# Root mean square norms by quarters: ScalarE's own sums under the root, gate product beside the squares, block 0 turned first

## The chip, the cores and the metric

One core of a Trainium2 chip runs the whole program. The metric is the device time of one launch in microseconds (us), the median of several runs. The engines are TensorE (PE; its weight loads are PEld), VectorE (DVE), ScalarE (ACT), GpSimd (POOL) and SyncE (SP), which issues most DMAs. TensorE writes only to PSUM, here eight banks of 128 x 512 f32, `PS[0]` to `PS[7]`.

## What is computed

Two transformer blocks over 256 tokens of width 1024, in f32, each a token mixer and then a mixture of experts (64 experts with 8 per token in the first, 32 with 2 per token in the second). What matters here are the norms around them:

```python
def rms_norm(x, g):
    return x * rsqrt(mean(x * x, axis=-1) + EPS) * g

# first block
x = x + gate0 * rms_norm(token_mixer(...), g_post_mix)      # norm 0
h = rms_norm(x, g_pre_ffn) * (1 + scale) + shift            # norm 1, then the router and the experts
x = x + gate1 * rms_norm(moe(h), g_post_ffn)                # norm 2
# second block
h = rms_norm(x, norm1_g) * (1 + scale1) + shift1            # norm 3
x = x + gate_mix * (mixed @ w_out)
h = rms_norm(x, norm2_g) * (1 + scale2) + shift2            # norm 4, then the router and the experts
x = x + gate_ffn * hier_moe(h)
return rms_norm(x, norm_f_g)                                # norm 5
```

## The kernel before

**Data.** `x` and `xn` hold the 256 tokens as two blocks `b` of 128 partitions by 1024 columns. A quarter is one block's half of 512 columns: quarter n is block n // 2, half n % 2. `hT` is the normalised and modulated `x` turned to features by tokens, eight slices `k` of 128 features; TensorE turns 128 x 128 pieces of `xn` into `PS[0]` to `PS[3]`, two slices to a bank, and VectorE (slices 0, 1, 4, 5) and ScalarE (2, 3, 6, 7) bring them to `hT` with scale `am` and shift `modc`. `gate` and `gate2` hold the gate rows broadcast over partitions.

**Order.** Each engine has its own program, written out by hand, and runs it in order. `Steps` (the helper `step`) adds to a semaphore behind an instruction and, unless told `wait=False`, makes the same engine wait for it before going on. Between engines there are named semaphores: `norm_in` (a block of `x` or `xn` is ready to be squared), `norm_sq` (ScalarE has squared it), `norm_ms` (VectorE has made mean + EPS), `norm_root` (ScalarE has the root), `xnorm_ready`, `modT` (a bank is turned), `ada_ready`, `y_done` (a quarter of the experts' sum is whole in PSUM), `stream_used`, `e1_gateup` and others (a weight buffer is free again).

**A norm of one block** goes: ScalarE squares 1024 columns and sums them (`norm`, L791), VectorE scales the sum and adds EPS (L1973), ScalarE takes the root (L793), VectorE the reciprocal (L1975). For a branch's norm (`add_branch`, norms 0 and 2) VectorE then multiplies by root and gate row (L1982) and adds to `x` (L1984), block after block; for a norm ahead of a projection (`modulated`, norms 1, 3, 4) it scales `x` into `xn` (L1997), both blocks, and TensorE turns both (L1208) when `xnorm_ready` says that the second is there. The last norm multiplies by its gain (L2336), and SyncE stores each block.

**The four places,** named as in the prediction: A, between the mixer's output projection (`mixed_out`, L1173) with three gate rows (`gate_rows`, L952, copied by ScalarE at L853) and the first router (L1225): norms 0 and 1. B, between the first layer's experts (L1378 closes the sums in PSUM, L2175 copies them out) and the second block's input projection (L1461): norms 2 and 3. C, between the second block's output projection (L1577; VectorE multiplies by the gate and adds at L1989, L1990) and its router: norm 4. D, behind the last expert: norm 5 and the store (L624).

**Weights.** SyncE issues the loads in order into a ring of twelve slots of 1 MB (`load_piece`, L536), later into three buffers (`load2`, L598), each when TensorE has used what lies there.

## Time and profile before

| | us |
|---|---|
| median of 3 runs | 1522.45 |
| lowest and highest | 1518.49, 1523.02 |
| profiled execution, first to last instruction (its span, and the only time that it has) | 1523.0 |
| TensorE busy | 1241.4 (82%) |
| weight loads of TensorE busy | 628.8 (41%) |
| VectorE busy | 360.9 (24%) |
| ScalarE busy | 181.5 (12%) |
| HBM read | 505.25 MB, 332 GB/s over the span |
| granted TensorE clock, mean | 0.901 |

The page is one execution as the hardware profiler saw it. A clock of 1.00 is 2.4 GHz and of 0.50 is 1.2 GHz. A timeline row gives the start, the time from first start to last end of the instructions merged in it, how many they are, and in brackets the idle time before them and who ended it. A stretch row gives busy time with instruction counts. The line numbers are those of the kernel before.

### The profile page before, as it was taken

How to read it: one execution, taken by the hardware profiler on the slowest of the kernel's cores; microseconds unless marked ns; L12 is line 12 of the kernel's file. 1: busy time of each engine (PE TensorE's matmuls, PEld its weight loads, DVE VectorE, ACT ScalarE, POOL GpSimd, SP SyncE). 2: the span in 40 equal slices, each digit the busy share in tenths (PEclk: the TensorE clock that was granted, in tenths of full speed). 3: DMA queues.
4: the chain of work that ended last, by engine and by line, in shares of the span. 5: the costliest groups of instructions: out<-in, count | busy, mean ns of one | idle time of the engine just before them, and what ended most of it. 6: DMA issues, size and time to landing. Idle time of an engine off the chain costs nothing.

```text
span 1523.0 us, 21627 instructions
## 1 busy us (share of the span) xinstructions
PE 1241.4 (82%) x8940; PEld 628.8 (41%) x8940; DVE 360.9 (24%) x932; ACT 181.5 (12%) x346; POOL 95.3 (6%) x125
## 2 busy tenths in 40 slices
PE   4999889899998989989796999887675675675764
PEld 2763335555555545545446544453221221221211
DVE  1498653611111101111113153323000000000002
ACT  1210200411111111111112012021000000000001
POOL 2398000000000000000001000000000000000000
PEclk9999979999999989999998999987788877778877
DMA  9875993269999999999967324445999999999993
GB/s 338 311 281 193 395 412 139 111 262 405 419 420 420 420 420 420 420 421 419 420 255 267 151 89 168 183 182 202 421 421 421 420 422 421 422 422 422 421 422 150
DMA packets 85980, 507.59 MB, mean 333 GB/s; under 512 B 8310, under 2 KB 9558, under 8 KB 36356
## 3 DMA queue, kind: packets, MB, share of 16 engines
q1 hardware_dynamic: 84804, 502.98, 80.9%
q0 software_dynamic: 944, 3.29, 0.7%
q8 instruction: 64, 1.05, 0.3%
q10 hardware_dynamic: 144, 0.07, 0.0%
q14 instruction: 24, 0.20, 0.0%
HBM read 505.25 MB, written 1.06 MB: 332 GB/s over the span
## 4 chain that ended last, share of the span: by engine, by line
PE 56%; DMA 32%; DVE 8%; SPq 2%; issue 2%; ACT 1%; DVEq 0%; ACTq 0%
DMA W<-in_w_expert_down 12%; DMA W<-in_w_expert_up 10%; PE PS L1432 10%; DMA W<-in_we_up 7%; PE PS L1300 5%; PE PS L1443 5%; PE PS L1287 4%; PE PS L1501 4%; PE PS L1597 3%; PE PS L1609 3%; PE PS L936 2%; DMA W<-in_w_ada 2%; PE PS L1173 2%; PE PS L1461 2%; PE PS L1577 2%; PE PS L1562 2%
## 5 line engine op out<-in xcount | busy, mean ns | idle before, releaser
L1597 PE MATMUL PS<-W,scr 128*32 128x512 f32 x1024 | 178.3, 862 | 121.6 <-DMA W<-in_w_expert_up 61.5
L1432 PE MATMUL PS<-W,scr 128*32 128x256 f32 (+1 forms) x2752 | 191.6, 400 | 30.9 <-DMA W<-in_we_up 26.6
L2098 DVE TENSOR_TENSOR scr<-scr,PS 128x256 f32<-128x256 f32 (+1 forms) x33 | 23.5, 712 | 664.5 <-PE PS L1597 386.4
L1432 PEld LDWEIGHTS PS<-W,scr 128*32 128x32 f32 (+1 forms) x2752 | 116.0, 120 | 113.8 <-issue 64.3
L1597 PEld LDWEIGHTS PS<-W,scr 128*32 128x32 f32 x1024 | 40.8, 150 | 257.5 <-issue 112.0
L1300 PE MATMUL PS<-scr 128*128 128x512 f32 x264 | 122.1, 605 | 2.5 <-ACT scr L824 2.5
L1609 PE MATMUL PS<-W,scr 128*32 128x512 f32 x512 | 72.7, 719 | 37.5 <-DMA W<-in_w_expert_down 36.6
L1287 PE MATMUL PS<-scr 128*128 128x128 bf16 x1584 | 93.8, 219 | 0.0
L1287 PEld LDWEIGHTS PS<-scr 128*128 128x128 bf16 x1584 | 91.2, 98 | 1.5 <-issue 1.1
L1443 PE MATMUL PS<-W,scr 128*32 128x512 f32 (+1 forms) x688 | 91.1, 596 | 0.7 <-DVE scr L2101 0.7
L813 ACT COPY scr<-PS 128x512 f32<-128x512 f32 x66 | 38.7, 586 | 437.8 <-PE PS L1287 437.8
L1300 PEld LDWEIGHTS PS<-scr 128*128 128x128 f32 x264 | 47.4, 189 | 67.7 <-issue 67.7
L824 ACT COPY scr<-PS 128x512 f32<-128x512 f32 x66 | 35.4, 589 | 211.9 <-PE PS L1609 128.2
L1501 PE MATMUL PS<-W,hT 128*128 128x512 f32 x128 | 56.0, 595 | 0.0
L936 PE MATMUL PS<-W,sc 128*32 128x512 f32 x384 | 48.3, 647 | 6.8 <-DMA W<-in_w_ada 6.6
L1609 PEld LDWEIGHTS PS<-W,scr 128*32 128x32 f32 x512 | 17.7, 128 | 86.3 <-DMA W<-in_w_expert_down 43.8
L669 POOL TENSOR_SCALAR scr<-scr,convw 128x256 f32<-128x256 f32 x44 | 44.4, 1010 | 4.3
L1443 PEld LDWEIGHTS PS<-W,scr 128*32 128x32 f32 (+1 forms) x688 | 24.5, 114 | 47.5 <-issue 44.1
L818 ACT ACTIVATE scr<-PS 128x256 f32<-128x256 f32 (+1 forms) x33 | 14.4, 435 | 219.3 <-PE PS L1597 142.5
L2101 DVE COPY scr<-PS 128x256 f32<-128x256 f32 (+1 forms) x33 | 16.1, 489 | 97.7 <-PE PS L1318 97.7
L1501 PEld LDWEIGHTS PS<-W,hT 128*128 128x128 f32 x128 | 24.0, 190 | 30.0 <-issue 30.0
L683 POOL DMA_DIRECT2D scr<-bias_by_distance x1 | 0.9, 925 | 558.1 <-DVEq L2180 558.1
(410 smaller groups left out, 1172.6 us busy)
## 6 DMA issues: line engine op xcount, KB each, us to landing
W<-in_we_gate SPq DMA_DIRECT2D x64, 1024.0 KB, 19.2
W<-in_we_up SPq DMA_DIRECT2D x64, 1024.0 KB, 17.4
W<-in_we_down SPq DMA_DIRECT2D x64, 1024.0 KB, 20.7
W<-in_w_expert_gate SPq DMA_DIRECT2D x64, 1024.0 KB, 18.8
W<-in_w_expert_up SPq DMA_DIRECT2D x64, 1024.0 KB, 19.0
W<-in_w_expert_down SPq DMA_DIRECT2D x64, 1024.0 KB, 19.3
W<-in_w_ada SPq DMA_DIRECT2D x10, 4096.0 KB, 18.6
W<-in_w_in SPq DMA_DIRECT2D x5, 4096.0 KB, 13.8
```

The source lines that it names most:

```text
L669: step(g.tensor_scalar(tmp, upad[:, i, :, j:j + ROW], convw[:, 4 * j + i:4 * j + i + 1], None, ALU.mult))
L813: a.copy(hTe[:, 4 * q:4 * q + 4, :], PS[4 + q][:].rearrange("p (k s) -> p k s", k=4)).then_inc(S["x_hTe"], 1)
L824: a.copy(Y[:, h * 512:(h + 1) * 512], PS[6 + h][:]).then_inc(S["x_Y"], 1)
L936: last = mm(PS[5 + h][32 * j:32 * j + 32, :], sc[:, 2 * j + kk, 30 - row:62 - row], ada_w[n][:, 2 * j + kk, h * 512:(h + 1) * 512], start= ...
L1173: last = mm(PS[2 * b + h][:, :], mixT[:, k, b * P:(b + 1) * P], w_o[:, k, h * 512:(h + 1) * 512], start=(k == 4), stop=(k == 3))
L1287: last = mm(PS[4 + k // 4][:, (k % 4) * P:(k % 4 + 1) * P], hs[:, part, b, k * P:(k + 1) * P], Sb[:, b, :], start=(q == 0), stop=(q == NB ...
L1300: last = mm(PS[2 * b + h][:, :], Ct[:, b * P:(b + 1) * P], Y[:, h * 512:(h + 1) * 512], start=False, stop=False)
L1432: m = mm(PS[4 + kind][at:at + size, 0:F1], hTe[:, k, at:at + size], piece_view((g, kind, j))[:, k, :], start=(k == 0), stop=(k == KD - 1))
L1443: m = mm(PS[6 + h][at:at + size, :], aT[:, c, at:at + size], piece_view((g, 2, j))[:, c, h * 512:(h + 1) * 512], start=(c == 0), stop=(c = ...
L1501: last = mm(PS[6 + n % 2][:, :], hT[:, k, b * P:(b + 1) * P], w2k[2 + half][:, k, h * 512:(h + 1) * 512], start=(k == 0), stop=(k == KD - 1))
L1597: m = mm(PS[bank][j * CAP2:(j + 1) * CAP2, :], hTe[:, k, j * CAP2:(j + 1) * CAP2], gu2[piece][:, j, kk, :], start=(k == 0), stop=(k == KD ...
L1609: m = mm(PS[6 + h][j * CAP2:(j + 1) * CAP2, :], aT[:, c, j * CAP2:(j + 1) * CAP2], dn2[piece][:, j, cc, h * 512:(h + 1) * 512], start=(c = ...
```

## The change

- Each root is made by ScalarE from two quarters. `root_of` squares a quarter with scale 1/32 (so that the sum is already a mean over 1024), adds EPS to the first sum by an Identity with a bias column `epsc`, squares the second quarter, and takes the root of its sum with the first as bias. VectorE's scaling step and `norm_sq`, `norm_ms` are gone in these norms.
- `norm_in` and the new `branch_in` count quarters, so a quarter is squared when it is there.
- In norm 0 VectorE multiplies the branch by the gate row into `branch` (the upper half of `hT`'s words) while ScalarE squares it; root and addition to `x` are then one fused instruction per quarter (`add_scaled`). In norm 2 the gate product takes the place of the copy out of PSUM, ScalarE squares `PS[0]` and `PS[1]` straight from the banks while VectorE takes quarters 2 and 3, and VectorE takes quarters 0 and 1 once block 0's root is there.
- `normalised(n, b)` scales one block and signals it. TensorE's `turn_rows(n, b)` turns one block: in A block 0 goes between gate rows 3 and 1, in C ahead of the last quarter of the output projection.
- In A block 0 goes through both norms on VectorE before the third quarter of the projection is read.
- `root_table` has ScalarE take a root of a constant ahead of norms 2, 4 and 5.
- The output is stored by quarters, in four DMAs of 256 KB.

```diff
--- before.py
+++ after.py
@@ -306,6 +306,12 @@
         sel16 = sel32[:, 0:16]
         ada_bias = [gate[:, n, :] for n in range(2)]
         onec = small[:, 340:341]
+        epsc, spare = small[:, 440:441], small[:, 441:442]
+
+        squares = [[[small[:, at:at + 1] for at in (448 + 8 * n + 4 * b, 449 + 8 * n + 4 * b)] for b in range(NB)] for n in range(2)]
+        halfway = [[small[:, 450 + 8 * n + 4 * b:451 + 8 * n + 4 * b] for b in range(NB)] for n in range(2)]
+        roots = [[small[:, 451 + 8 * n + 4 * b:452 + 8 * n + 4 * b] for b in range(NB)] for n in range(2)]
+        branch = hT_words[:, D:2 * D]
         cvec = small[:, 376:400].rearrange("p (v k) -> p v k", v=3)
 
         rowd = {"post_mix": scr[:, 4096:5120], "post_ffn": scr[:, 11264:12288]}
@@ -619,10 +625,11 @@
 
             over_loads(2, ("w_expert_gate_2", "w_expert_up_2", "w_expert_down_2"))
 
-            for b in range(NB):
-                sp.wait_ge(S["out_ready"], b + 1)
-                sp.dma_start(out[0][b * P:(b + 1) * P, :], xn[:, b, :]).then_inc(S["stored"], 16)
-            sp.wait_ge(S["stored"], 16 + 16 * NB)
+            for n in range(4):
+                b, q = n // 2, slice(n % 2 * 512, n % 2 * 512 + 512)
+                sp.wait_ge(S["out_ready"], n + 1)
+                sp.dma_start(out[0][b * P:(b + 1) * P, q], xn[:, b, q]).then_inc(S["stored"], 16)
+            sp.wait_ge(S["stored"], 16 + 16 * 4)
 
 
         @block.gpsimd
...
@@ -785,12 +793,25 @@
                 mod_columns(bank, i, b, s, n == 2)
 
 
-            def norm(n, src):
-                for b in range(NB):
-                    act.wait_ge(S["norm_in"], 2 * n + b + 1)
-                    step(a.activation(hT_words[:, 0:D] if n < 2 else ada_rows[:], src[:, b, :], ACT.Square, accum_out=st[:, 24 + b:25 + b]), S["norm_sq"])
-                    act.wait_ge(S["norm_ms"], 2 * n + b + 5)
-                    step(a.activation(st[:, 26 + b:27 + b], st[:, 26 + b:27 + b], ACT.Sqrt), S["norm_root"])
+            def root_of(n, b, quarters, ready, first):
+
+                unused = hT_words[:, 0:512] if n < 2 else ada_rows[:, 0:512]
+                for h in range(2):
+                    act.wait_ge(S[ready], first + h)
+                    step(a.activation(unused, quarters[2 * b + h][:, 0:512], ACT.Square, scale=1.0 / 32, accum_out=squares[n % 2][b][h]))
+                    if h == 0:
+                        step(a.activation(halfway[n % 2][b], squares[n % 2][b][0], ACT.Identity, bias=epsc))
+                step(a.activation(roots[n % 2][b], squares[n % 2][b][1], ACT.Sqrt, bias=halfway[n % 2][b]), S["norm_root"])
+
+            x_quarter = [x[:, n // 2, n % 2 * 512:n % 2 * 512 + 512] for n in range(4)]
+            xn_quarter = [xn[:, n // 2, n % 2 * 512:n % 2 * 512 + 512] for n in range(4)]
+
+            def root_of_x(n, nth, b):
+                root_of(n, b, x_quarter, "norm_in", 4 * nth + 2 * b + 1)
+
+            def root_table():
+
+                step(a.activation(spare, onec, ACT.Sqrt))
 
             def split_h(L, part):
 
...
@@ -875,10 +898,11 @@
                 act.wait_ge(S["sh_gateup"], b + 1)
                 step(a.activation(sg_sh[:, b, :], PS[6 + b][:, 0:F1], ACT.Silu), S["sh_sg"], wait=False)
             experts(1, NG1, F1, 2)
-            norm(2, xn)
-
-
-            norm(3, x)
+            root_table()
+            root_of(2, 0, PS, "y_done", 1)
+            root_of(2, 1, PS, "branch_in", 5)
+            for b in range(NB):
+                root_of_x(3, 1, b)
             odd_banks_of_h(1, 1, 0, 2)
 
             for h in range(HEADS2):
...
@@ -1193,21 +1221,24 @@
                 last.then_inc(S["hmT"], 1)
             pe.wait_ge(S["mixT_m"], 2)
             mixed_out(0)
+            def turn_rows(n, b):
+
+                pe.wait_ge(S["xnorm_ready"], 2 * n + b + 3)
+                for k in range(KD):
+                    part = xn[:, b, k * P:(k + 1) * P] if n == 1 else every_kd(xn[:, b, :])[:, k, :]
+                    last = tr(PS[k // 2][:, (k % 2) * T + b * P:(k % 2) * T + (b + 1) * P], part, ident[:])
+                    if b and k % 2:
+                        last.then_inc(S["modT"], 1)
+
             pe.wait_ge(S["gates_made"], 1)
             gate_rows(2, (5, 6))
             gate_rows(3, (4, 7))
+
+            pe.wait_ge(S["branch_in"], 4)
+            turn_rows(0, 0)
             pe.wait_ge(S["ada_ready"], 5)
             gate_rows(1, (5, 6))
-
-            def modulated(n, src):
-
-                pe.wait_ge(S["xnorm_ready"], n + 3)
-                for k in range(KD):
-                    for b in range(NB):
-                        part = src[:, b, k * P:(k + 1) * P] if n == 1 else every_kd(src[:, b, :])[:, k, :]
-                        last = tr(PS[k // 2][:, (k % 2) * T + b * P:(k % 2) * T + (b + 1) * P], part, ident[:])
-                    if k % 2:
-                        last.then_inc(S["modT"], 1)
+            turn_rows(0, 1)
 
             def part_of_h(n, k):
 
...
@@ -1447,7 +1477,8 @@
             experts(1, NG1, F1, gate_and_up1, down1)
 
 
-            modulated(1, xn)
+            for b in range(NB):
+                turn_rows(1, b)
 
             def loaded2(i):
                 pe.wait_ge(S[f"stream2_loaded{i % 2}"], 16 * (i // 2 + 1) if i != 5 else 48)
@@ -1577,9 +1608,11 @@
                     last = mm(PS[4 + n][:, :], hT[:, k, b * P:(b + 1) * P], w2k[5][:, k, h * 512:(h + 1) * 512],
                               start=(k == 0), stop=(k == KD - 1))
                 last.then_inc(S["stream2_used"] if n == 3 else S["proj_mm"], 1)
-
-
-            modulated(2, xn)
+                if n == 2:
+                    turn_rows(2, 0)
+            turn_rows(2, 1)
+
+
             routed(2, 2, wr2, 36)
             pe.wait_ge(S["zraw_ready"], 1)
             ranks(2, E2)
@@ -1961,40 +1994,35 @@
             over_rows(1, E1)
             sort_keys()
 
-            norms = []
-
-            def next_norm():
-                norms.append(len(norms))
-                return norms[-1]
-
-            def root_mean_square(n, b):
-
-                dve.wait_ge(S["norm_sq"], 5 + 2 * n + b)
-                step(v.tensor_scalar(st[:, 26 + b:27 + b], st[:, 24 + b:25 + b], 1.0 / D, EPS, ALU.mult, ALU.add), S["norm_ms"])
-                dve.wait_ge(S["norm_root"], 5 + 2 * n + b)
-                step(v.reciprocal(st[:, 26 + b:27 + b], st[:, 26 + b:27 + b]))
-
-            def add_branch(gate_row):
-
-                n = next_norm()
-                for b in range(NB):
-                    root_mean_square(n, b)
-                    step(v.scalar_tensor_tensor(out=xn[:, b, :], in0=xn[:, b, :], scalar=st[:, 26 + b:27 + b],
-                                                in1=gate_row, op0=ALU.mult, op1=ALU.mult))
-                    step(v.tensor_tensor(x[:, b, :], x[:, b, :], xn[:, b, :], ALU.add), S["norm_in"])
+            ROOTS = [(0, 0), (1, 0), (0, 1), (1, 1)] + [(n, b) for n in range(2, 6) for b in range(NB)]
+
+            def inverse_root(n, b):
+
+                dve.wait_ge(S["norm_root"], 5 + ROOTS.index((n, b)))
+                inverse = st[:, 26 + b:27 + b]
+                step(v.reciprocal(inverse, roots[n % 2][b]))
+                return inverse
+
+            def add_scaled(n, b, product):
+
+                inverse = inverse_root(n, b)
+                for h in range(2):
+                    q = slice(h * 512, h * 512 + 512)
+                    step(v.scalar_tensor_tensor(out=x[:, b, q], in0=product[:, q], scalar=inverse, in1=x[:, b, q],
+                                                op0=ALU.mult, op1=ALU.add), S["norm_in"])
 
             def add_product(gate_row, n, bank):
 
                 b, q = n // 2, slice(n % 2 * 512, n % 2 * 512 + 512)
                 step(v.tensor_tensor(xn[:, b, q], bank[:], gate_row[:, q], ALU.mult))
-                step(v.tensor_tensor(x[:, b, q], x[:, b, q], xn[:, b, q], ALU.add), S["norm_in"] if n % 2 else None)
+                step(v.tensor_tensor(x[:, b, q], x[:, b, q], xn[:, b, q], ALU.add), S["norm_in"])
+
+            def normalised(n, b):
+
+                step(v.tensor_scalar(xn[:, b, :], x[:, b, :], inverse_root(n, b), None, ALU.mult), S["xnorm_ready"])
 
             def modulated(n, blk, sec, vec, gain):
 
-                norm = next_norm()
-                for b in range(NB):
-                    root_mean_square(norm, b)
-                    step(v.tensor_scalar(xn[:, b, :], x[:, b, :], st[:, 26 + b:27 + b], None, ALU.mult), S["xnorm_ready"] if b else None)
                 step(v.scalar_tensor_tensor(out=am[:, 0, :], in0=modc[:, blk, sec + 1, :, vec], scalar=1.0,
                                             in1=gain, op0=ALU.add, op1=ALU.mult), S["am_ready"])
                 for k in (0, 1, 4, 5):
@@ -2146,8 +2174,10 @@
                 for h in range(2):
                     dve.wait_ge(S["stream_used"], AT["w_out"] + 1) if b and h else dve.wait_ge(S["proj_mm"], 17 + 2 * b + h)
                     q = slice(h * 512, (h + 1) * 512)
-                    step(v.tensor_tensor(xn[:, b, q], PS[2 * b + h][:], rowv[:, q], ALU.add), S["norm_in"] if h else None)
-            add_branch(gate[:, 0, :])
+                    step(v.tensor_tensor(xn[:, b, q], PS[2 * b + h][:], rowv[:, q], ALU.add), S["branch_in"])
+                    step(v.tensor_tensor(branch[:, q], xn[:, b, q], gate[:, 0, q], ALU.mult))
+                add_scaled(0, b, branch)
+                normalised(1, b)
             modulated(0, 0, 2, 0, ffn_cols[:, FFN_G1, :])
 
             mixer_gate(1, 7)
@@ -2170,12 +2200,16 @@
             make_ranks(1, E1)
             experts(1, NG1, F1, 2)
 
-            for n in range(4):
+            for n in (2, 3, 0, 1):
                 dve.wait_ge(S["y_done"], n + 1)
-                step(v.tensor_copy(xn[:, n // 2, n % 2 * 512:n % 2 * 512 + 512], PS[n][:]), S["norm_in"] if n % 2 else None)
-            add_branch(gate[:, 1, :])
-
-
+                if n == 0:
+                    dve.wait_ge(S["norm_root"], 5 + ROOTS.index((2, 0)))
+                q = slice(n % 2 * 512, n % 2 * 512 + 512)
+                step(v.tensor_tensor(xn[:, n // 2, q], PS[n][:], gate[:, 1, q], ALU.mult), S["branch_in"] if n > 1 else None)
+            for b in range(NB):
+                add_scaled(2, b, xn[:, b, :])
+            for b in range(NB):
+                normalised(3, b)
             modulated(1, 1, 0, 2, cols[:, C_N1:C_N1 + 8])
             dve.sem_inc(S["x2_ready"], 1)
             for q in range(4):
@@ -2270,8 +2304,8 @@
             for n in range(4):
                 dve.wait_ge(S["proj_mm"], 23 + n) if n < 3 else dve.wait_ge(S["stream2_used"], 6)
                 add_product(gate2[:, 0, :], n, PS[4 + n])
-
-
+                if n % 2:
+                    normalised(4, n // 2)
             modulated(2, 1, 2, 2, ffn_cols[:, FFN_G2, :])
             dve.wait_ge(S["router_mm"], 2)
             zz = tmpr.rearrange("p b e -> p (b e)")[:, 0:72].rearrange("p (b n) -> p b n", b=NB)
@@ -2330,11 +2364,12 @@
                 add_product(gate2[:, 1, :], n, PS[n])
 
             dve.wait_ge(S["poolw_loaded"], 32)
-            norm = next_norm()
             for b in range(NB):
-                root_mean_square(norm, b)
-                step(v.scalar_tensor_tensor(out=xn[:, b, :], in0=x[:, b, :], scalar=st[:, 26 + b:27 + b], in1=rowf,
-                                            op0=ALU.mult, op1=ALU.mult), S["out_ready"])
+                inverse = inverse_root(5, b)
+                for h in range(2):
+                    q = slice(h * 512, h * 512 + 512)
+                    step(v.scalar_tensor_tensor(out=xn[:, b, q], in0=x[:, b, q], scalar=inverse, in1=rowf[:, q],
+                                                op0=ALU.mult, op1=ALU.mult), S["out_ready"])
 
 
 
```

## Rows read from the trace of the kernel before

**Rows 1.** The page's part 4: shares of the chain that ended last, by engine.

```profile
PE 56%; DMA 32%; DVE 8%; SPq 2%; issue 2%; ACT 1%; DVEq 0%; ACTq 0%
```

**Rows 2.** Stretches: busy us (instructions) of PE, PEld, DVE, ACT, POOL, granted clock, DMA, GB/s.

```profile
345.00:440.00 95.00, 95.00 (x1130) 54.04 (x1131) 14.12 (x59) 15.39 (x29) 0.00 (x0) 1.00 1.00 414
1060.00:1500.00 440.00, 285.31 (x1856) 89.31 (x1852) 22.45 (x48) 19.89 (x35) 0.00 (x0) 0.79 1.00 418
```

**Rows 3.** Timeline of SyncE's DMA queue: start us, us with waits between, instructions.

```profile
269.79 36.36 SPq L536 DMA_DIRECT2D W<-in_we_up  x2
```

**Rows 4.** Groups by shape: line, engine, operation, tiles, count, busy us, mean ns, idle before.

```profile
L895 ACT ACTIVATE scr<-scr 128x512 f32<-128x512 f32 x8 | 4.4, 618 | 4.8 <-DVE scr L2231 4.8
L888 ACT ACTIVATE scr<-scr,small 128x256 f32<-128x256 f32 x8 | 4.1, 508 | 0.3
L818 ACT ACTIVATE scr<-PS 128x256 f32<-128x256 f32 x25 | 9.6, 383 | 76.8 <-PE PS L1432 76.8
L793 ACT ACTIVATE small<-small 128x1 f32<-128x1 f32 x12 | 2.4, 203 | 14.6 <-DVE small L1973 14.5
L791 ACT ACTIVATION_READ_ACCUMULATOR ada_rows<-x 128x1 f32 x6 | 1.1, 187 | 0.0
L1982 DVE SCALAR_TENSOR_TENSOR xn<-xn,small,gate 128x1024 f32<-128x1024 f32 x4 | 5.1, 1284 | 0.1
L1984 DVE TENSOR_TENSOR x<-x,xn 128x1024 f32<-128x1024 f32 x4 | 4.9, 1226 | 0.1
```

**Rows 5.** Timelines of VectorE, ScalarE and TensorE in A: start us, us, idle before.

```profile
268.54 0.69 DVE L2149 TENSOR_TENSOR xn<-PS,scr 128x512 f32<-128x512 f32 x1 [2.74 <-PE PS L1173]
278.41 0.75 DVE L1997 TENSOR_SCALAR xn<-x,small 128x1024 f32<-128x1024 f32 x1
273.08 1.07 ACT L853 COPY gate<-PS 128x512 f32<-128x512 f32 x2
268.27 3.60 PE L952 MATMUL PS<-ada_rows,scr 128*128 128x512 f32 x8
274.21 1.98 PE L952 MATMUL PS<-ada_rows,scr 128*128 128x512 f32 x4 [2.34 <-ACT gate L853]
279.22 3.53 PE L1208 MATMUL PS<-ident,xn 128*128 128x128 f32 x16 [3.03 <-DVE xn L1997]
```

**Rows 6.** Stretches behind the waits of A and C, columns as in rows 2.

```profile
279.20:290.00 10.80, 10.78 (x69) 9.74 (x70) 6.27 (x20) 5.67 (x11) 0.00 (x0) 0.84 0.07 28
1014.70:1032.00 17.30, 15.61 (x86) 15.09 (x86) 8.09 (x32) 7.68 (x14) 0.00 (x0) 0.50 0.32 134
```

**Rows 7.** Timeline of TensorE: sixteen turnings at full clock, ahead of C.

```profile
977.23 1.97 PE L1569 MATMUL PS<-ident,xn 128*128 128x128 f32 x16 [2.36 <-DVEq L2265]
```

**Rows 8.** Timelines of VectorE, ScalarE and TensorE in B.

```profile
797.30 2.87 DVE L2175 COPY xn<-PS 128x512 f32<-128x512 f32 x4 [8.94 <-PE PS L1378]
802.03 0.16 DVE L1975 RECIPROCAL small<-small 128x1 f32<-128x1 f32 x1 [1.68 <-ACT small L793]
800.43 1.28 ACT L793 ACT_TABLE_LOAD   x1 [0.53 <-DVE small L1973]
811.44 3.67 PE L1208 MATMUL PS<-ident,xn 128*128 128x128 f32 x16 [13.53 <-DVE xn L1997]
```

**Rows 9.** The stretch in which TensorE's full clock returns in B, columns as before.

```profile
815.00:816.00 1.00, 1.00 (x5) 0.86 (x5) 0.30 (x1) 0.84 (x2) 1.00 (x2) 0.80 1.03 410
```

**Rows 10.** DMA issues of 792.2 to 792.6 us: tiles, KB each, us to landing.

```profile
W<-in_w_in SPq DMA_DIRECT2D x1, 4096.0 KB, 13.8
```

**Rows 11.** Timeline of TensorE in C: turning and router.

```profile
1014.71 3.67 PE L1208 MATMUL PS<-ident,xn 128*128 128x128 f32 x16 [6.13 <-DVE xn L1997]
1018.18 6.88 PE L1225 MATMUL PS<-gate,hT 128*128 128x36 f32 x32
```

**Rows 12.** Timeline of VectorE in D: last add, second output.

```profile
1513.52 0.69 DVE L1990 TENSOR_TENSOR x<-x,xn 128x512 f32<-128x512 f32 x1
1518.72 1.28 DVE L2336 SCALAR_TENSOR_TENSOR xn<-x,small,gate 128x1024 f32<-128x1024 f32 x1
```

More of the change, by code:

```diff
@@ L639, in _ @@
             step(g.memset(onec, 1.0), wait=False)
+            step(g.memset(epsc, EPS), wait=False)
             step(g.memset(gate_parts, 0.0), wait=False)
@@ L895, in _ @@
                 step(a.activation(zg[:, b, q], zg[:, b, q], ACT.Sigmoid), S["zg_ready"], wait=False)
-            norm(4, x)
+            root_table()
+            for b in range(NB):
+                root_of_x(4, 2, b)
             odd_banks_of_h(2, 1, 2, 2)
@@ L905, in _ @@
             experts(2, NG2, F2, 4)
-            norm(5, x)
+            root_table()
+            for b in range(NB):
+                root_of_x(5, 3, b)
         @block.tensor
@@ L1379, in experts @@
                         .then_inc(S["y_done"], 1)
-            modulated(0, xn)
             routed(1, 0, wr, E1)
@@ L2171, in _ @@
             experts(1, NG1, F1, 2)
-            for n in range(4):
+            for n in (2, 3, 0, 1):
                 dve.wait_ge(S["y_done"], n + 1)
-                step(v.tensor_copy(xn[:, n // 2, n % 2 * 512:n % 2 * 512 + 512], PS[n][:]), S["norm_in"] if n % 2 else None)
-            add_branch(gate[:, 1, :])
+                if n == 0:
+                    dve.wait_ge(S["norm_root"], 5 + ROOTS.index((2, 0)))
+                q = slice(n % 2 * 512, n % 2 * 512 + 512)
+                step(v.tensor_tensor(xn[:, n // 2, q], PS[n][:], gate[:, 1, q], ALU.mult), S["branch_in"] if n > 1 else None)
+            for b in range(NB):
+                add_scaled(2, b, xn[:, b, :])
+            for b in range(NB):
+                normalised(3, b)
             modulated(1, 1, 0, 2, cols[:, C_N1:C_N1 + 8])
```

6 lines of the change are left out of this document (4 added, 2 removed).

## The prediction

> **What bounds the kernel now.** The page's shares of the chain that ended last come first [rows 1]: TensorE has 56% of it, DMA 32%, VectorE 8%. An average hides where each rules, so the second view is the table of stretches [rows 2]. In 345 to 440 us TensorE is never idle and the DMA engines are full too (414 GB/s); in 1060 to 1500 us DMA moves 418 GB/s at a share of 1.00, and TensorE works only 285 of 440 us. Nothing in the change touches those stretches. It touches the four places between them where TensorE waits for a root mean square: before the first router (A, 268 to 283 us), after the first experts (B, 797 to 815), before the second router (C, 1008 to 1018) and at the end (D, from 1514). So two questions decide: how much shorter each gets, and whether the weight stream that follows starts earlier with it. SyncE's queue answers the second [rows 3]: after its load at 269.79 it stands for 36 us until the shared expert's matmuls free a slot. Only then does it go on; every later load is issued on such an event of TensorE. In layer two likewise, where the fourth load waits for the first gate matmuls. The streams are full but started by TensorE, so I pass every gain through whole.
>
> **Prices of pieces** [rows 4]. VectorE on 512 columns of f32: 0.69 [rows 5], next start 0.035 later. A 1024 column product with a per-row scalar is 1.28; a plain 1024 column add is 1.23 against 0.69 for 512, so the second half costs 0.53, and a fused half costs 1.28 - 0.53 = 0.75. ScalarE on 512 columns: 0.62 to 0.63, and reading the accumulator (0.19, some 0.09 of it beside the Square) brings a quarter to 0.73. The tiny Sqrt is 0.20; the new ones have a bias column, which the trace has not at this size. On 256 columns 0.508 with a bias and accumulation stands against 0.383 without; the bound is 0.20 to 0.33 and I take 0.30, near the upper row, because the new form is the one with the column. From the last quarter ready to the end of VectorE's reciprocal: 0.03 + 0.73 + 0.03 + 0.30 + 0.10 + 0.16 = 1.35. When two quarters come close together, the first one's Identity (0.30) stands in front of the second Square: 1.66. The old step went Square, VectorE scaling, Sqrt, reciprocal, so two of the crossings between the engines go, and all but the last quarter's Square lies beside other work.
>
> **A** [rows 5]. Before: last quarter of the projection at 268.54 (the others 2.74 + 0.69 = 3.43 apart ahead of it), four roots in series between 1024 column operations, last `xn` at 279.16, turning 279.22 to 282.75. After, on VectorE: quarter 1 is added 261.68 to 262.37 and multiplied to 263.10 (it used to idle there), root to 263.72, two fused halves to 265.29, root of x 1.66 later to 266.96, `xn` of block 0 at 267.75. This stands in front of quarter 2, whose product bank was ready at 265.11; it is read from 267.79. Quarter 3 is then read 269.24 to 269.93 rather than 268.54, multiplied to 270.65, root 271.28, halves 272.85. ScalarE has the gate copies (1.07) behind the root of block 0's twin, 271.05 to 272.12, so they are done in time; x's quarters: Square 272.15, Identity, Square, Sqrt at 274.30, reciprocal 274.56, `xn` of block 1 at 275.35. TensorE meanwhile: gate rows 268.27 to 271.87, block 0 turned, gate row 1 (1.9, it waited for the copies at 272.12), ready for block 1 about 274.8. It is idle 0.6 us instead of 2.3 and 3.0. Now the clock: the turning in A ran at half clock, 3.53 for 16, as the granted clock of the stretch shows (0.84 in all) [rows 6], while at full clock 16 take 1.97 [rows 7]. Without the long idle I take full clock: turning ends 275.4 + 1.0 = 276.4, VectorE and ScalarE bring `hT` pieces from 276.0 on as fast as the router wants them (0.45 each), and the router starts near 276.6. Gain 282.7 - 276.6 = 6.1; if the clock falls all the same, 5.2.
>
> **B** [rows 8]. Before: TensorE idle 13.53, from 797.91 to 811.44, then 3.67 of turning at half clock, L1461 at 815.1. In it: four copies out of PSUM (2.87 from 797.30), a table load of 1.28, four roots in series. After: ScalarE squares banks 0 and 1 themselves from 797.3, root of block 0 at 799.45; VectorE takes quarters 2, 3 to 799.2, then 0, 1 to 800.97 (0 waits 0.35 for the root); block 1's root 801.63; fused halves 801.2 to 802.73 and 802.97 to 804.5; roots of x on ScalarE 804.15 and 806.33; `xn` block 0 at 805.48, block 1 at 807.38. TensorE turns block 0 in the shadow and block 1 from 807.43 to 809.26 at half clock. That is 5.9 earlier. Full clock came back 4.4 us after the restart at 811.44 [rows 8, 9]; with the restart in two pieces L1461 may run up to 1.3 us of work longer at half, against 0.35 before. I take off 0.5: gain 5.4. L1461's weights are next to be late: issued at 792.29, 13.8 us to landing [rows 10], 806.1; cover of 3.2 us.
>
> The load of the square root's table goes out of the path in B, C and D; `root_table` does it after the last copy of the experts or gates. The trace prices it at 1.28: VectorE's whole wait at 802.03, with load, Sqrt and crossings, is 1.68 [rows 8]. The Trainium skill (ScalarE: Activation LUTs, What ACT_TABLE_LOAD costs) gives 2.66 us for a switch, with a drain of 1.38 behind the load. By that the three hidden loads would be worth 4.1 us more. The trace doesn't agree: 1.68 less 1.28 leaves 0.40, and no room for a drain beside a Sqrt of 0.20.
>
> **C** [rows 11]. Before: TensorE's last quarter ends at 1008.58 (6.13 of idle before 1014.71), VectorE takes it at 1008.69, TensorE turns from 1014.71 to 1018.38. After: a quarter of this projection takes 6.9, so block 0 is whole 13.7 before the last quarter ends, and two adds, root and scaling (1.4 + 1.4 + 0.8) have its `xn` ready some 3 us before TensorE gets to the turning ahead of the last quarter. At full clock it costs 0.98, so the last quarter comes at 1009.67: the one thing that the change delays. Then two VectorE steps to 1011.09, root 1012.44, `xn` 1013.23, eight turns from 1013.26. At half clock they end 1015.1, gain 3.3. The moved turning also makes the last projection slot free 1 us later for an expert load that is wanted only behind the router; nothing.
>
> **D** [rows 12]. VectorE's last add ends at 1514.21 in both. Before, the second output ends at 1520.0 and the span 3.0 later. After, block 0's root is long there: 1514.41, halves to 1515.98, block 1's root (Sqrt at 1515.30) costs only the reciprocal, 1516.18, halves to 1517.75. Gain 2.25. The last store is 256 KB in place of 512: at the some 400 GB/s of the loads 0.65 less. Gain 2.9. Four stores in place of two cost four issues, 0.78 apart, hidden. POOL's extra memset lies at the start beside 6 us of the first load.
>
> **Sum.** 6.1 + 5.4 + 3.3 + 2.9 = 17.7. The profiled execution's span is 1523.0, 0.55 above the median of the three times, 1522.45. So 1505.3 as a span and 1504.8 as a median.
>
> **Rivals.** (1) The clock holds in C. Before, it fell during 6 us of idle and stayed half through the turning and the router (0.50) [rows 6]; TensorE now rests 3.7 us. If it stays up, eight turns save 0.85, the router's 6.7 [rows 11] becomes 3.4, and the later zero matmuls give 0.5: 4.6 more, 1500.2. For it speaks the shorter rest, against it that in A it fell on a rest of 3.0 after another of 2.3 [rows 5]. Chance 0.23. (2) A's gain is swallowed by the weight stream, as would be if it ran on its own from 269.79. The standing queue speaks against it. 1504.8 + 6.1 = 1510.9, chance 0.14. (3) Roots are dearer: VectorE now stands before full PSUM banks for a root (A, quarter 2; B, quarter 0) and each root has four ScalarE steps. At 1 us more per root, A loses 4, B 3, C and D 1 each: 1513.8, chance 0.07. (4) Slower: if Square or Identity shared no table with Sqrt, each of the 12 roots would load two tables. 24 x 1.28 = 30.8 against 17.7 gives 1535.5; from 14 loads on the path it is slower. Against it stands the trace: twelve Square and Sqrt pairs with three loads, and Identities behind them with none. Chance 0.02. (5) The change does nothing here, because something unseen ends the waits: 1522, chance 0.03.
>
> **How the numbers follow.** The forecast has 0.51. The range goes from 1498 (the clock case at 1500.2, less 2 for the spread of runs, which was 1518.5 to 1523.0) to 1512 (rival 2, plus 1). It leaves out rivals 3 to 5 and some of the rest. A measurement of this kernel can tell about 0.3%, 4.6 us. Faster: forecast and rivals 1, 2, 3, 0.95; same 0.03; slower 0.02.
>
> **What would show it.** In the timeline: router start 6 us earlier with TensorE idle under 1 us in A; no table load between 797 and 808, 1009 and 1013, or after 1508; L1461 5 to 6 us earlier; granted clock 1.00 in A; SyncE's first load after the long stand earlier by A's gain, and the last store 3 us closer. A Square of over 0.8 or an Identity of over 0.4 would break the root's price. The prediction is wrong if DMA stays as late as before in 345 to 440.

## The result, and the profile after

The changed kernel takes 1507.59 us in the median of four runs (1506.09 to 1508.7), beside 1522.74 (1518.49 to 1524.71) for four runs of the kernel before: a ratio of 0.990, with a 95% interval of 0.9884 to 0.9916. It is faster by 15.2 us. A later measurement gave 0.9888 (0.9869 to 0.9906), 1507.22 against 1523.98, thus 16.8 us. The span of the profiled execution and its chain (the page's first line and part 4):

```profile
span 1506.9 us, 21655 instructions
PE 54%; DMA 34%; DVE 7%; SPq 2%; issue 1%; ACT 1%; DVEq 0%; ACTq 0%
```

That execution took 1508.7 us as a run, 1.8 more than its span; the same 1.8 lies around every span here that has a time. VectorE's share of the chain went from 8% to 7%, TensorE's from 56% to 54%, and DMA's rose to 34% [rows 1].

A ledger of both pairs of profiles that there are, by landmarks on TensorE that exist in all of them (us; the stretches add up to the span):

| stretch | before | before again | after | after again |
|---|---|---|---|---|
| start to gate rows 2, 3 | 268.27 | 268.38 | 268.08 | 266.70 |
| A: to the router | 14.28 | 14.41 | 8.50 | 8.50 |
| router to first gather | 23.08 | 22.95 | 22.97 | 22.97 |
| first experts, to the closing matmuls | 491.26 | 493.12 | 493.61 | 493.26 |
| B: to the input projection | 18.02 | 18.02 | 12.22 | 12.35 |
| to VectorE's first quarter of C | 173.18 | 173.87 | 172.93 | 173.02 |
| C: to the router | 30.09 | 29.77 | 26.92 | 26.92 |
| router to zero matmuls | 13.87 | 11.07 | 13.87 | 13.85 |
| to the first gate matmul | 10.59 | 10.80 | 10.27 | 10.40 |
| second experts, to the closing matmuls | 465.39 | 465.39 | 465.31 | 465.32 |
| D: to the end | 14.97 | 15.02 | 12.22 | 12.21 |

So the four places gave 5.78 + 5.80 + 3.17 + 2.75 = 17.5 in the first pair and 5.91 + 5.67 + 2.85 + 2.81 = 17.2 in the second. The spans as wholes differ by 16.1 and 17.3, because the stretches between the places vary too.

**A.** Timelines of VectorE and TensorE in the kernel after (start us, us, idle before in brackets):

```profile
261.48 0.69 DVE L2177 TENSOR_TENSOR xn<-PS,scr 128x512 f32<-128x512 f32 x1 [1.09 <-PE PS L1201]
263.62 1.54 DVE L2011 SCALAR_TENSOR_TENSOR x<-hT,small,x 128x512 f32<-128x512 f32 x2
266.69 0.16 DVE L2003 RECIPROCAL small<-small 128x1 f32<-128x1 f32 x1 [1.54 <-ACT small L804]
267.68 0.69 DVE L2177 TENSOR_TENSOR xn<-PS,scr 128x512 f32<-128x512 f32 x1
269.13 0.69 DVE L2177 TENSOR_TENSOR xn<-PS,scr 128x512 f32<-128x512 f32 x1
274.49 0.75 DVE L2022 TENSOR_SCALAR xn<-x,small 128x1024 f32<-128x1024 f32 x1
268.08 3.60 PE L980 MATMUL PS<-ada_rows,scr 128*128 128x512 f32 x8
271.51 1.05 PE L1229 MATMUL PS<-ident,xn 128*128 128x128 f32 x8
272.40 1.88 PE L980 MATMUL PS<-ada_rows,scr 128*128 128x512 f32 x4
275.29 1.16 PE L1229 MATMUL PS<-ident,xn 128*128 128x128 f32 x8 [1.01 <-DVE xn L2022]
276.58 3.75 PE L1256 MATMUL PS<-scr,hT 128*128 128x64 f32 x32
```

VectorE multiplies quarter by quarter where it idled, then stands 1.5 us for block 0's second root while quarter 2 waits in PSUM (read at 267.68). TensorE has 1.01 us of idle left, where it had 2.34 and 3.03 [rows 5]. Eight turnings take 1.05 and 1.16, against 3.53 for sixteen. The granted clock, by stretches (columns as in rows 2):

```profile
279.20:290.00 10.80, 10.80 (x59) 6.79 (x57) 8.66 (x26) 6.16 (x11) 0.00 (x0) 1.00 0.06 26
1005.00:1023.00 18.00, 16.27 (x78) 13.68 (x77) 10.75 (x42) 7.93 (x15) 0.00 (x0) 0.50 0.35 149
```

Behind A it is now 1.00 (0.84 before), behind C still 0.50 [rows 6]. The new instructions by shape, as in rows 4:

```profile
L801 ACT ACTIVATE ada_rows<-x 128x512 f32<-128x512 f32 x12 | 7.6, 630 | 67.9 <-DVE x L2018 67.3 <-DVE x L2011 0.5
L804 ACT ACTIVATE small<-small 128x1 f32<-128x1 f32 x12 | 3.5, 294 | 0.4
L2011 DVE SCALAR_TENSOR_TENSOR x<-xn,small,x 128x512 f32<-128x512 f32 x4 | 3.0, 751 | 0.1
```

A quarter's Square is 0.63, the root with a bias 0.29 (0.20 without), a fused half 0.75.

**B.** ScalarE, VectorE and TensorE:

```profile
789.53 1.28 ACT L814 ACT_TABLE_LOAD   x1
795.41 0.29 ACT L804 ACTIVATE small<-small 128x1 f32<-128x1 f32 x1
795.84 1.42 DVE L2208 TENSOR_TENSOR xn<-PS,gate 128x512 f32<-128x512 f32 x2 [0.41 <-ACT small L804]
802.75 0.16 DVE L2003 RECIPROCAL small<-small 128x1 f32<-128x1 f32 x1 [0.96 <-ACT small L804]
802.94 0.76 DVE L2022 TENSOR_SCALAR xn<-x,small 128x1024 f32<-128x1024 f32 x1
793.16 1.03 PE L1409 MATMUL PS<-ones,zeros 128*128 128x512 bf16 x4
801.84 3.70 PE L1229 MATMUL PS<-ident,xn 128*128 128x128 f32 x16 [7.65 <-DVE xn L2022]
```

The table load starts right behind the last expert's copies, 3.6 us before the matmuls at 793.16 that close the sums; [rows 8] has it inside. VectorE waits 0.41 for block 0's root ahead of quarter 0. TensorE idles 7.65 where it idled 13.53.

**C**, TensorE:

```profile
991.77 1.05 PE L1229 MATMUL PS<-ident,xn 128*128 128x128 f32 x8
1003.47 1.97 PE L1229 MATMUL PS<-ident,xn 128*128 128x128 f32 x8 [3.77 <-DVE xn L2022]
1005.23 6.88 PE L1256 MATMUL PS<-gate,hT 128*128 128x36 f32 x32
```

Block 0 is turned in 1.05 at full clock, ahead of the last quarter. The idle behind that quarter is 3.77 (6.13 in [rows 11]), the eight turnings then take 1.97 at half clock, and the router 6.88 as before.

**D**, VectorE:

```profile
1500.18 0.69 DVE L2018 TENSOR_TENSOR x<-x,xn 128x512 f32<-128x512 f32 x1
1502.68 0.16 DVE L2003 RECIPROCAL small<-small 128x1 f32<-128x1 f32 x1
1502.88 1.54 DVE L2371 SCALAR_TENSOR_TENSOR xn<-x,small,gate 128x512 f32<-128x512 f32 x2
```

The last output ends at 1504.42, 2.48 before the end of the span, where [rows 12] had 3.0. SyncE's queue answers the row in [rows 3]; the load starts at the same place and the stand is 5.9 us shorter:

```profile
269.60 30.48 SPq L542 DMA_DIRECT2D W<-in_we_up  x2
```

### The profile page after: what moved, and what is told of

Read it like the earlier page. It is cut to its first block, busy times and chain, and to the rows that moved or that the text cites. A ratio compares the mean times of both kernels' runs of the same rounds, so it can differ in the third digit from the quotient of the medians.

```text
span 1506.9 us, 21655 instructions
## 1 busy us (share of the span) xinstructions
PE 1238.2 (82%) x8940; PEld 624.6 (41%) x8940; DVE 357.9 (24%) x926; ACT 190.0 (13%) x385; POOL 95.4 (6%) x126
## 3 DMA queue, kind: packets, MB, share of 16 engines
q8 instruction: 64, 1.05, 0.3%
HBM read 505.25 MB, written 1.06 MB: 336 GB/s over the span
## 4 chain that ended last, share of the span: by engine, by line
PE 54%; DMA 34%; DVE 7%; SPq 2%; issue 1%; ACT 1%; DVEq 0%; ACTq 0%
DMA W<-in_w_expert_down 12%; DMA W<-in_w_expert_up 11%; PE PS L1462 9%; DMA W<-in_we_up 9%; PE PS L1331 5%; PE PS L1473 5%; PE PS L1532 4%; PE PS L1318 4%; PE PS L1630 3%; PE PS L1642 3%; PE PS L964 2%; DMA W<-in_w_ada 2%; PE PS L1608 2%; PE PS L1593 2%; PE PS L1492 2%; PE PS L1502 2%
## 5 line engine op out<-in xcount | busy, mean ns | idle before, releaser
L2129 DVE COPY scr<-PS 128x256 f32<-128x256 f32 (+1 forms) x33 | 16.1, 489 | 97.7 <-PE PS L1349 97.7
```

## Experiments

The measure is the local stretch of the ledger, since the times of one kernel spread by up to 10 us. Not every comparison with after was made on one chip, but after's own two profiles agree within 0.13 in every local stretch of the four places. B needs more care: in eight profiles with the same B, after's two among them, it took 12.08 to 12.36. In all of them VectorE's last row there ends 10.54 behind the closing matmuls; what varies is how long TensorE's turnings take (3.55 to 3.89 for sixteen), thus when the clock comes back. Where the two differ, that row is the better measure. Six of the changed versions have a single run; all that is said of them rests on one profile each.

**Does the weight stream swallow A's gain?** In the first pair A's 6.1 us (with the start's 0.2) arrived at the closing matmuls as 3.7. The kernel before was profiled again.

> The kernel before, unchanged, for a second profile. Measure: the first layer's expert stage, from the first gather matmul behind the router to the four closing matmuls of the sums. It took 305.63 to 796.89 = 491.3 us in the profile of before and 299.55 to 793.16 = 493.6 in that of after, so 2.3 of the 6.1 us that A gave were gone by its end. Theory: the weight stream varies by a few us from run to run, and this repeat lies anywhere from 489 to 495, 1 us or more off 491.3. Rival: the stream runs partly on its own and swallows part of every shift that comes before it; then this repeat is within 0.5 of 491.3.

The repeat took 493.1 for the first experts, 1.9 off the first profile and near the 493.6 of after. The eleven other profiles have these instructions too: 490.1, 490.8, 492.0, 492.1, 492.5, 492.6, 493.1, 493.1, 493.3, 493.4, 493.6. The stretch varies by 3.5 us for one and the same work, and the first profile of before was on its short side. So nothing was swallowed that can be told from this spread: the two profiles of before average 492.2, the twelve others 492.5. Between router and gather the shift passed whole (22.97 against 23.08 and 22.95), and `whole_squares`, which from gate rows to gather took 8.35 us longer than after, needed 492.1 for its experts, in the middle of the fourteen.

**Table load.** `root_table()` is left out in its three places.

```diff
-            root_table()
```

> After, without root_table: the table of the square root is loaded at the first Sqrt of B, C and D, on the path. Theory: a load costs 1.28 and nothing behind it. B: the load stands before block 0's first root, +1.28, of which the wait of quarter 0 takes all: router side of B +1.3. C: the first Sqrt belongs to block 0, whose turning has 3 us of cover, so 0. D: block 0's root has 2 us of cover, so 0. In all +1.3 us on 1507.6. Rival (a switch costs 2.66 with its drain): B +2.7, C and D 0 to 0.7 each, in all +2.7 to +4.

B was 13.28, +1.06, and VectorE's last row there ended 11.72 behind the closing matmuls, +1.18. C's stretch 26.45 and D's 12.15 did not grow. (C's is 0.47 shorter because the clock fell later, in the middle of block 1's turning; TensorE's idle ahead of it is 3.77 as in after.) ScalarE and VectorE in B:

```profile
793.33 1.28 ACT L804 ACT_TABLE_LOAD   x1
794.62 0.30 ACT L804 ACTIVATE small<-small 128x1 f32<-128x1 f32 x1
795.05 1.42 DVE L2205 TENSOR_TENSOR xn<-PS,gate 128x512 f32<-128x512 f32 x2 [1.62 <-ACT small L804]
```

Load and root follow each other with 0.01 between, and VectorE waits 1.62 where it waited 0.41, 1.21 more. So a switch costs the 1.28 of its load, and no drain shows. The median was 1508.91 (ratio 0.9894, 0.9864 to 0.9923), in which 1.3 can't be told from nothing. The rival with a drain is out.

**Whole squares.** Each root waits for its second quarter before the first Square.

```diff
-                    act.wait_ge(S[ready], first + h)
+                    act.wait_ge(S[ready], first + 1)
```

> After, but each root waits for both quarters before its first Square (same instructions, only the wait moved). Theory: after the last quarter the first Square and its Identity lie on the path, 1.08 for quarters far apart and 0.76 for a close pair. A: four roots in series, +3.7, router at 12.2 (and perhaps the clock falls in the longer idle, +1 more). B +0.8, C +1.05, D +0.5. In all +6.1. Rival: VectorE is what the chain waits for and the order of squaring matters little, under +2 in all.

A 12.65 (+4.15), B 13.36 (+1.14), C 27.99 (+1.07), D 12.70 (+0.48): 6.8 against 6.1. And the clock, which the expectation had in brackets, did fall. VectorE's last row and TensorE in A:

```profile
279.11 0.75 DVE L2022 TENSOR_SCALAR xn<-x,small 128x1024 f32<-128x1024 f32 x1
275.96 2.86 PE L980 MATMUL PS<-ada_rows,scr 128*128 128x512 f32 x4 [2.17 <-ACT gate L874]
279.92 1.97 PE L1229 MATMUL PS<-ident,xn 128*128 128x128 f32 x8 [1.10 <-DVE xn L2022]
281.68 6.93 PE L1256 MATMUL PS<-scr,hT 128*128 128x64 f32 x32
```

Block 1's row ends 10.83 behind the start of the gate rows rather than 7.16, so the chain of roots grew by 3.67. Behind it, block 1's turning at half clock adds 0.48. The router, 3.75 in after, took 6.93, and router to gather went from 22.97 to 27.17, 4.2 us more. So 3.67 us of a longer root chain cost 8.35 in and behind A, and 4.68 of that, more than half, is the clock. In all four places and behind the router of A this one moved wait costs 11.0 us; the one run took 1520.05.

**ScalarE's own sums undone.** The sum of the two quarters goes back to VectorE.

```diff
...
-                    if h == 0:
-                        step(a.activation(halfway[n % 2][b], squares[n % 2][b][0], ACT.Identity, bias=epsc))
-                step(a.activation(roots[n % 2][b], squares[n % 2][b][1], ACT.Sqrt, bias=halfway[n % 2][b]), S["norm_root"])
+                act.wait_ge(S["norm_ms"], 5 + ROOTS.index((n, b)))
+                step(a.activation(roots[n % 2][b], halfway[n % 2][b], ACT.Sqrt), S["norm_root"])
...
+                step(v.scalar_tensor_tensor(out=halfway[n % 2][b], in0=squares[n % 2][b][0], scalar=EPS, in1=squares[n % 2][b][1],
+                                            op0=ALU.add, op1=ALU.add), S["norm_ms"])
```

> After, but the sum of the two quarters and EPS goes back to VectorE, in one small instruction with norm_sq and norm_ms around it; ScalarE then takes a root without a bias and makes no Identity. Measure: the four stretches as in the other runs (after: A 8.50, B from closing matmuls to projection 12.22, C from VectorE's first quarter to the router 26.92, D from closing matmuls to the end 12.22). Theory: where VectorE stands free, a crossing costs only 0.24 (0.10 + 0.16 + 0.10 less the bias's 0.09), so A +0.5, C +0.25. Where VectorE is busy, ScalarE is held in front of the next Square until VectorE gets there: B +1.45, D +1.1. In all +3.3. Rival: a crossing is dear everywhere, 0.5 or more per root, A +2.

A +0.42, B +1.95, C +0.24, D +1.27, in all 3.9 against 3.3. Where VectorE is free a crossing costs a quarter of a us. Where it is busy, ScalarE is the one that stands. In B:

```profile
791.27 0.19 ACT L803 ACTIVATION_READ_ACCUMULATOR ada_rows<-PS 128x1 f32 x1
793.60 0.20 ACT L806 ACTIVATE small<-small 128x1 f32<-128x1 f32 x1 [2.14 <-DVE small L2004]
791.77 1.54 DVE L2021 SCALAR_TENSOR_TENSOR x<-xn,small,x 128x512 f32<-128x512 f32 x2
793.35 0.16 DVE L2004 SCALAR_TENSOR_TENSOR small<-small 128x1 f32<-128x1 f32 x1
```

ScalarE has block 1's squares at 791.46 and waits 2.14 us until VectorE has done its two fused halves and comes to the sum at 793.35. The gain of own sums is thus in B and D. B came out 0.5 above the expectation. VectorE's last row there ends 12.35 behind the closing matmuls, 10.54 in after, 1.81 more where 1.45 was expected: 0.36 lies in its chain, which I had added up too short, and the rest is within what B varies by.

**Gate product behind the root in A.**

```diff
-                    step(v.tensor_tensor(branch[:, q], xn[:, b, q], gate[:, 0, q], ALU.mult))
-                add_scaled(0, b, branch)
+                add_late(0, b, gate[:, 0, :])
```

`add_late` multiplies a half by root and gate row and then adds it to `x`.

> After, but in A the gate product is made behind the root, by halves (multiply by root and gate, then add to x), as four instructions per block rather than two, and none beside the squares. Theory: A +1.5 (block 1's own two extra instructions of 0.7; block 0's cost is mostly given back, as quarter 3 no longer waits for quarter 2's product), so 10.0. Rival: both blocks' extra instructions are on the path, +2.9, 11.4.

10.51, +2.0: between the two theories, nearer to the first. The product beside the squares is worth 2 us in A.

**Block 0 turned ahead, A.** Gate row 1 first, then block 0's turning.

> After, but in A TensorE makes gate row 1 before it turns block 0. Measure: from the start of gate rows 2 and 3 to the router, 8.50 us in after. Theory: block 1's scaled row is the last to come (TensorE waits 1.0 us for it even now), so where block 0 is turned doesn't matter: it waits for the gate copies 0.3 us, and block 0's eight turns then take up the wait. 8.5 within 0.3. Rival: the turning ahead is worth its 0.9 us or holds the clock, 9.4 or more.

8.51. In A the turning ahead is worth nothing; block 1's row is what TensorE waits for.

**Block 0 turned ahead, C.**

```diff
-                if n == 2:
-                    turn_rows(2, 0)
-            turn_rows(2, 1)
+            for b in range(NB):
+                turn_rows(2, b)
```

> After, but in C block 0 is turned behind the last projection quarter, together with block 1's wait. Theory: the eight turns fit into the wait for block 1's root (3.8 us idle), so the router starts no later, and the last quarter ends 0.9 us earlier: the router of C starts 0.9 us EARLIER than in after, counted from the end of the projection's third quarter. Turning ahead is then a small loss. Rival: turning ahead is what keeps the wait short; behind it the router starts 1 to 2 us later. Clock: theory expects it to fall here too.

25.56, 1.36 less than after. TensorE:

```profile
995.96 1.05 PE L1229 MATMUL PS<-ident,xn 128*128 128x128 f32 x8
999.90 1.28 PE L1229 MATMUL PS<-ident,xn 128*128 128x128 f32 x8 [2.89 <-DVE xn L2021]
```

The turning fits into the wait (2.89 left), so ahead of the last quarter it only delays. 0.9 is that, and 0.5 came from the clock, which fell later: eight turnings took 1.28 rather than 1.97.

**The clock held in C.**

```diff
+            for _ in range(4):
+                mm(PS[4][:, :], zeros[:], outer(ones[:], 4), start=True, stop=True)
             turn_rows(2, 1)
```

> After, with four matmuls of zeros by ones (512 columns, f32, into the free bank 4) between block 0's turning with the last quarter and block 1's turning in C, 3.4 us of the 3.8 that TensorE idles there. Their result is overwritten. Theory of the forecast's first rival: the granted clock stays 1.00 through turning and router, the turning saves 0.9, the router goes from 6.7 to 3.4 and the later zero matmuls give 0.5: in all 4.6 us less, 1503. Rival: the router's matmuls of 36 columns let the clock fall to 0.50 anyway within a few us, and the gain is 1 to 2 us.

TensorE's turning ahead of C, then TensorE in C, and two stretches of the router (clock is the column after the engines' busy times):

```profile
966.72 3.45 PE L1600 MATMUL PS<-ident,xn 128*128 128x128 f32 x16 [2.36 <-DVEq L2301]
999.58 3.60 PE L1614 MATMUL PS<-ones,zeros 128*128 128x512 f32 x8
1003.52 1.16 PE L1229 MATMUL PS<-ident,xn 128*128 128x128 f32 x8 [0.34 <-DVE xn L2024]
1004.80 4.70 PE L1256 MATMUL PS<-gate,hT 128*128 128x36 f32 x32
1006.00:1007.00 1.00, 1.00 (x11) 1.00 (x10) 0.01 (x1) 0.98 (x2) 0.00 (x0) 1.00 1.03 434
1008.00:1009.00 1.00, 1.00 (x7) 1.00 (x6) 0.00 (x0) 0.00 (x0) 0.00 (x0) 0.50 0.99 418
```

C 26.44 and router to zero matmuls 11.68: 2.7 less in all, not 4.6. The 0.5 in C is no more than `no_table_ahead` had unheld (26.45), when the clock fell late by itself; the 2.2 behind the router's start stands out among the changed versions, of which no unheld one came under 13.85 there. The turnings ran at full clock and the router began so, but in 1008 the clock was at 0.50 with TensorE busy all the time. The median was 1503.16, with times from 1499.18 to 1509.03 (ratio 0.9861, 0.982 to 0.9902); this profile's stretch ahead of C was 2.5 longer and its first experts 3.5 shorter than after's, so its span doesn't show the gain. The 2.5 is the clock too: sixteen turnings there took 3.45, where they took 1.97 at full clock [rows 7], and the 64 matmuls ahead of them 29.4 rather than 27.7. `no_table_ahead` and `a_product_late` had such a fall there as well (175.3 and 175.5 for that stretch, 172.9 to 173.9 in the eleven others). The repeat of before shows that the clock also comes up by itself in this router. Its timeline and stretches:

```profile
1017.37 3.32 PE L1208 MATMUL PS<-ident,xn 128*128 128x128 f32 x16 [6.13 <-DVE xn L1997]
1020.52 4.08 PE L1225 MATMUL PS<-gate,hT 128*128 128x36 f32 x32
1016.00:1017.00 1.00, 0.00 (x0) 0.00 (x0) 0.60 (x2) 0.20 (x1) 0.00 (x0) 0.50 0.97 410
1021.00:1022.00 1.00, 1.00 (x11) 1.00 (x11) 0.23 (x1) 0.98 (x3) 0.00 (x0) 1.00 1.06 451
1024.00:1025.00 1.00, 1.00 (x6) 1.00 (x7) 0.32 (x2) 0.00 (x0) 0.00 (x0) 0.50 0.00 0
```

Half clock ahead of the turning, full in the router (4.08 rather than 6.88), half again behind it. The profiles of the same kernel differ by 2.8 us in this alone.

**A shorter A, and what it brings with the others.** VectorE scales block 0's row between quarters 2 and 3.

```diff
                     step(v.tensor_tensor(branch[:, q], xn[:, b, q], gate[:, 0, q], ALU.mult))
+                    if b and not h:
+                        normalised(1, 0)
                 add_scaled(0, b, branch)
-                normalised(1, b)
+            normalised(1, 1)
```

> After, but in A VectorE scales block 0's row between quarters 2 and 3 of the projection rather than ahead of quarter 2. Theory: quarter 3 is then read when TensorE has it, 0.78 earlier, and the whole chain of block 1 with it; TensorE waits 1.0 us for that chain, so A goes from 8.50 to 7.72. Rival: ScalarE, which then has block 0's second root and block 1's first Square close together, holds block 1 up, and A stays at 8.3 to 8.5.

7.72, as worked out.

> After with the order of a_dve_order in A and the turning of c_turn_behind in C. Theory: A 7.7, C 25.6 to 26.0, in all 1.7 to 2.1 us below after in the same call. Rival: nothing that can be measured over the spread of the times.

A 7.72, C 25.55, so 2.15 less. The second experts took 466.1 rather than 465.3 and gave 0.8 of it back; why is open (the two other versions with block 0's turning behind the last quarter had 465.6 and 466.2, all the rest 465.1 to 465.5). The median was 1507.01 (1501.63 to 1508.8), that of after, measured beside it, 1507.22 (1504.33 to 1508.34): no difference that can be told.

> order_and_behind with matmuls of zeros by ones in TensorE's waits: eight ahead of the first turning in B (6.9 us of 7.7 idle) and three ahead of block 1's turning in C (2.6 us of 2.9), into the free bank 4. Theory: in B the clock stays 1.00, block 1's turning takes 0.9 rather than 1.8, B 12.2 to 11.4. In C the clock stays through the turning and the first us of the router and then falls, router 4.7 rather than 6.9, in all some 2.5 to 3 us below order_and_behind. Rival: the clock comes and goes by chance in C as the two profiles of before showed (router 6.88 and 4.08), and the held kernel is 1 us better on the median at most.

B 11.84 (0.5 less, not the expected 0.8), C 25.56, router to zero matmuls 10.71 rather than 14.00. TensorE in B, then in C:

```profile
801.12 1.09 PE L1229 MATMUL PS<-ident,xn 128*128 128x128 f32 x8 [0.79 <-DVE xn L2025]
803.04 1.09 PE L1229 MATMUL PS<-ident,xn 128*128 128x128 f32 x8 [0.82 <-DVE xn L2025]
998.49 2.74 PE L1615 MATMUL PS<-ones,zeros 128*128 128x512 f32 x6
1002.84 3.73 PE L1256 MATMUL PS<-gate,hT 128*128 128x36 f32 x32
```

The turnings in B are at full clock (1.09 each), and the router in C takes 3.73. The median is 1505.25 (1503.81 to 1505.31), 2.0 below after's, measured beside it. The ratios to before, 0.9877 (0.9858 to 0.9896) and 0.9888 (0.9869 to 0.9906), overlap, so the profile shows the version as better and the times don't settle it. The unchanged kernel, measured once more beside these, did this:

> After, unchanged: a second profile and more times. Theory: the local stretches repeat (A 8.5, B 12.2, C 26.9, D 12.2, each within 0.2 but for the clock in C), while the first layer's expert stage lies anywhere from 490 to 494 and the start of gate rows 2 and 3 anywhere from 264.5 to 269.5; the ratio to before is 0.990 within 0.0015, thus 15 us. Rival: the true gain is that of the local stretches alone, 17.7, ratio 0.9884.

Local stretches repeat within 0.13. The ratio, 0.9888, lies between what the two theories name and doesn't part them. The ledger gives 17.5 and 17.2 for the four places, and the second pair's spans differ by 17.3, the first's by 16.1. So the gain of the whole kernel is 15 to 17 us by every measure, and that the stretches between the places take nothing of it is likely, not shown.

## Why the prediction was right, point by point

- **What bounds, and whether gains pass.** Right. Rival 2 fell with the repeat of before, although the first pair alone would have spoken for it with 2.3 us.
- **Prices of pieces.** Quarter Square with its reading 0.73, root with a bias 0.29 (0.30 taken), fused half 0.75. These made the sums of A and D hold to 0.3.
- **A, 6.1.** 5.8 and 5.9. The chain on VectorE came within 0.1 of the worked one: with the start shifted by 0.19, `xn` of block 1 was due at 275.16 and ended at 275.24. The router started 0.2 later than taken, and before it had started at 282.55, not 282.7. TensorE was idle for 1.01, not under 1. The clock held, as taken. `whole_squares` shows what a fall can cost here, 0.48 in the turning and 4.2 behind the router's start; the prediction had priced it at 0.9, because it counted the turnings but not the router behind them. That it held because the idle time is short is an argument from two versions, one with 1.01 of idle and one with 2.17 and 1.10.
- **B, 5.4.** 5.8 and 5.7. VectorE's chain fits to 0.05 (block 1's row due 807.38, or 803.65 when shifted by 3.73, found 803.70). The 0.5 taken off for the clock was mostly not needed: the turning was over, and the clock back, about when the input projection began. (The 4.4 us that the prediction gives for the clock's return before is 4.0 by its own row: a mean clock of 0.80 in 815 to 816 puts it at 815.4, behind a restart at 811.44.) The hidden table load was worth 1.1 to 1.2, in B alone: in C and D it lay beside other work when put back. The Trainium skill's 2.66 (ScalarE: Activation LUTs, What ACT_TABLE_LOAD costs) isn't borne out. How much of B comes from squaring the banks directly and from the gate product in place of the copies, no run shows.
- **C, 3.3.** 3.2 and 2.9, clock at half. That block 0's turning ahead delays the last quarter by 0.98 was seen and counted, rightly. What the prediction didn't ask is whether it would have fitted into the wait behind that quarter: it does, and `c_turn_behind` and `order_and_behind` are shorter by 1.4, of which 0.9 is the delay and 0.5 a later fall of the clock.
- **D, 2.9.** 2.8: 2.23 up to the last output (2.25 taken) and 0.52 behind it (0.65 taken for the smaller store, which no run tries alone).
- **The sum.** 17.7 worked out, 17.5 and 17.2 in the four places. The forecast of 1504.8 is the median that was known of before, 1522.45, less 17.7; the measured 1507.59 is 2.8 above it. Of that, 0.3 is the median of before, which a fourth run moved to 1522.74. The rest, 2.5, is that the medians of four runs each lie only 15.2 apart, with an interval of 12.8 to 17.7; the second pair of medians lies 16.8 apart. In sum the terms were off by 0.2 to 0.5, so most of the 2.5 arose outside the four places, in runs that spread by 3 to 6 us, and that it was no larger is in part luck. One reading was wrong but without effect: the span of 1523.0 was set beside the medians as if it were a time, 0.55 above them, while a time is 1.8 more than its span. It cancels, since the sum was taken off the median all the same.
- **Rival 1, the clock in C.** It didn't happen in after. Held by hand it gave 2.2 behind the router's start in one kernel and 3.3 in another, of the 3.8 expected there; the clock was not steady in this router.
- **Rivals 3 to 5** didn't occur: the roots cost what was worked out, no table was loaded between Square and Sqrt, and the waits went.

## What to carry to other kernels

When a chain of small steps between two engines lies in a wait of TensorE, cut it by pieces so that only the last piece's step is left behind the last arrival, and let one engine make the whole scalar, so that it needn't wait for a busy partner. Before counting a stage moved ahead as a gain, ask whether it fits into the wait anyway. And judge a change of 1% by stretches between landmarks: here one profile against one other would have given a false finding of 2.3 us, while the four changed stretches of after repeated to 0.13.

## What the runs showed of the hardware

- The first experts' stage, with the same instructions, took 490.1 to 493.6 us in fourteen profiles, the second one 465.1 to 466.2. The start (to gate rows 2 and 3) took 264.6 to 269.2; in the profiles of `own_sums_undone` (264.6) and `whole_squares` (269.0) the first ada matmul, which waits for its weights, stands at 20.53 and 22.38, and by 46 us the later one is 4.4 behind.
- In C the clock changed while TensorE was busy: from 0.50 to 1.00 and back within 5 us of router and turning in one profile of before, while in the other it stayed at 0.50 through both. In `c_clock_held` it fell in the third us of the router, though TensorE had rested only 0.34 us since 999.58.
- A small activation with a bias column takes 0.29, without one 0.20.
- TensorE at half clock takes 6.88 for the router's 32 matmuls of 36 columns and 3.73 at full clock, so a cold clock behind a wait can cost as much as the wait that was cut.
